# Opening of a two-model kernel in four steps of two channel blocks

## What is computed

```python
c_act = silu(c)                                   # c: one vector of 1024
mod = c_act @ w_ada[l] + b_ada[l]                 # 1024 -> 6 * 1024
sh_m, sc_m, gt_m, sh_f, sc_f, gt_f = split(mod, 6)
h = rms_norm(x, g_pre_mix[l]) * (1.0 + sc_m) + sh_m
proj = h @ w_in[l]                                # 1024 -> 3656
mq, mk, mv, dq, dk, dv, qi, ki, wi = split(proj)  # 512 * 6, 512, 64, 8
...                                               # rope on q and k; moba attention on m*,
...                                               # top-k scores from qi, ki, wi, then dsa attention on d*
x = x + gt_m * rms_norm(concat(o_moba, o_dsa) @ w_out[l])
...                                               # then a convolutional gated feed-forward
```

## Time and profile before

| | us |
|---|---|
| median of 3 runs | 2640.02 (2638.87 to 2648.0) |
| the profiled execution | 2643.63 |
| its span, first to last instruction | 2641.8 |
| PE busy | 2504.3 (95%) |
| DVE busy | 1746.1 (66%) |
| ACT busy | 1073.3 (41%) |
| POOL busy | 446.3 (17%) |
| mean granted TensorE clock | 0.984 |
| DMA read | 409.68 MB, 155 GB/s over the span |

### The profile page before, as it was taken

How to read it: one execution, slowest core, us unless ns; L and a number is a source line. 1 busy time by engine, 2 the same in 40 slices (tenths; PEclk the granted TensorE clock), 3 DMA queues, 4 the chain that set the end, 5 groups by cost and what they waited for, 6 DMA issues and landing times.

```text
span 2641.8 us, 35187 instructions
## 1 busy us (share of the span) xinstructions
PE 2504.3 (95%) x13498; PEld 2092.2 (79%) x13498; DVE 1746.1 (66%) x2572; ACT 1073.3 (41%) x1818; POOL 446.3 (17%) x462
## 2 busy tenths in 40 slices
PE   4898999989999999999989999999999999999998
PEld 3677997678988878878658888888888888777997
DVE  6976886966995785776875464665565765345454
ACT  3455544456554222226745322224322224334543
POOL 1101111001121111113842112101112110000111
PEclk9999999999999999999999999999999999999999
DMA  7644785534774453551102244352343343222462
GB/s 304 208 172 146 272 307 204 206 129 175 244 266 152 159 199 135 189 185 57 63 32 72 88 170 145 144 187 89 135 168 120 141 181 117 91 73 76 156 196 95
DMA packets 118294, 413.02 MB, mean 156 GB/s; under 512 B 13552, under 2 KB 17776, under 8 KB 118128
## 3 DMA queue, kind: packets, MB, share of 16 engines
q1 hardware_dynamic: 117568, 409.06, 44.5%
q10 hardware_dynamic: 560, 1.72, 0.2%
HBM read 409.68 MB, written 1.05 MB: 155 GB/s over the span
## 4 chain that ended last, share of the span: by engine, by line
PE 61%; DVE 3%; ACT 2%; POOL 1%; issue 1%; DVEq 0%; POOLq 0%; ACTq 0%
PE ps L1102 18%; PE ps L1104 18%; PE ps L1103 18%; PE ps L1318 2%; PE ps L1295 1%; PE ps L1255 1%; PE ps L1286 1%; DVE sl L1672 1%; PE ps L1266 1%; POOL ap L2194 1%; POOL X L2155 1%; ACT F L1440 1%; DVE F L1789 1%; DVE mjunk L1686 0%; ACT sh L1381 0%
## 5 line engine op out<-in xcount | busy, mean ns | idle before, releaser
L1102 PE MATMUL ps<-hH,sh 128*128 128x256 f32 (+1 forms) x2560 | 843.0, 329 | 8.7 <-DVE hL L1760 3.5
L1103 PE MATMUL ps<-hL,sh 128*128 128x256 f32 (+1 forms) x2560 | 836.2, 327 | 0.0
L1104 PE MATMUL ps<-hH,sl 128*128 128x256 f32 (+1 forms) x2560 | 836.1, 327 | 0.0
L1672 DVE TENSOR_TENSOR sl<-raw,sh 128x1024 fp32r<-128x1024 f32 x534 | 655.1, 1251 | 123.3 <-ACT sh L1381 122.3
L1381 ACT ACTIVATE sh<-raw 128x1024 fp32r<-128x1024 f32 x534 | 540.3, 1039 | 392.5 <-PE ps L1104 326.3
L1686 DVE CUSTOM_DVE_ANT_0 mjunk<-raw,cB,V 128x1024 bf16<-128x1024 f32 x384 | 545.6, 1421 | 30.3 <-DMA C<-in_cst 8.3
L1102 PEld LDWEIGHTS ps<-hH,sh 128*128 128x128 f32 x2560 | 481.7, 188 | 61.7 <-issue 10.6
L1103 PEld LDWEIGHTS ps<-hL,sh 128*128 128x128 f32 x2560 | 482.8, 189 | 48.8 <-issue 1.7
L1104 PEld LDWEIGHTS ps<-hH,sl 128*128 128x128 f32 x2560 | 480.6, 188 | 48.1
L2167 POOL TENSOR_TENSOR uLl<-F,uHh 128x256 fp32r<-128x256 f32 (+1 forms) x132 | 166.8, 1264 | 988.9 <-ACT uHh L1561 853.5
L1102 PE MATMUL ps<-sh,uHh 128*128 128x512 f32 x792 | 316.5, 400 | 15.2 <-DVE sl L1672 15.1
(11 more groups left out here) (170 smaller groups left out, 2254.7 us busy)
## 6 DMA issues: line engine op xcount, KB each, us to landing
raw<-in_w SPq DMA_DIRECT2D x756, 512.0 KB, 4.5
raw<-in_w SPq DMA_DIRECT2D x16, 256.0 KB, 3.8
cB<-in_rpb SPq DMA_DIRECT2D x64, 64.0 KB, 2.6
X<-in_x ACTq DMA_DIRECT2D x1, 1024.0 KB, 11.7
X<-in_ctx SPq DMA_DIRECT2D x1, 1024.0 KB, 7.9
out<-X SPq DMA_DIRECT2D x2, 512.0 KB, 2.6
raw<-in_w SPq DMA_DIRECT2D x2, 288.0 KB, 5.5
cB<-in_c ACTq DMA_DIRECT2D x1, 512.0 KB, 5.5
```

The source lines that it names most:

```text
L1102: self.e.matmul(out, lh, rh, start=start, stop=False)
L1103: self.e.matmul(out, lh, rl, start=False, stop=False)
L1104: return self.e.matmul(out, ll, rh, start=False, stop=stop)
L1672: self.e.tensor_tensor(lo[:, 0:w], raw[:, 0:w], hi[:, 0:w].bitcast(F32), ALU.subtract).then_inc(self.sems["w_lo"], 1)
```

## The change

The 16 modulation sums, the blocks of `h` and the start of the projection are interleaved in four steps kp = 0 to 3. Each step takes four sums (2kp, 2kp + 1, 8 + 2kp, 9 + 2kp), makes two channel blocks of `h` for both token tiles (`hpair`), and runs the units of these two channels for column blocks 6, 0 and 1. x is transposed once, before scale and shift, into `xT` (it lies in the space of `O1`). Block 7 comes behind block 0. The load of x moves from third in ACT's queue to first in SP's. Rates and the order of the index steps change; the `idx` steps of both tiles now come ahead of all `rank` steps, in layer 1 as well.

```diff
-RATES = {"proj0": 0.8, "proj1": 0.65, "att": 0.0, ...
+RATES = {"proj0": 1.0, "proj1": 0.65, "att0": 0.75, "att1": 0.0, ...
@@ mixer
-        begun = {cb: blocks(cb) for cb in (6, 7)}
-        for i in range(2):
+        begun = {cb: blocks(cb) for cb in (6, 7)} if l else self.opening(hid, blocks)
+        for i in range(2 if l else 0):
...
-        for cb in (6, 7, 0, 1, 2, 3, 4, 5):
+        for cb in (6, 7, 0, 1, 2, 3, 4, 5) if l else (6, 0, 7, 1, 2, 3, 4, 5):
...
-                    if at in (2, 4) and pending:
+                    if (at in (2, 4) or not l and cb in (7, 2)) and pending:
                         pending.pop(0)()
                     self.pace()
...
+                if not l:
+                    pending.insert(0, go)      # the turn of block 7 goes first
+                    continue
...
-        self.rate = RATES["att"]
+        self.rate = RATES[f"att{l}"]
+    def opening_mods(self, kp):
+        for u in (2 * kp, 2 * kp + 1, 8 + 2 * kp, 9 + 2 * kp):
+            self.jobs.remove(("w_ada", 0, u))
+            self.add("place", unit=self.unit(False, [("w_ada", 0, None, u * 128, D)], ("w_ada", 0, u)))
+
+    def opening(self, hid, blocks):
+        cbs = (6, 0, 1)
+        banks = {cb: [self.bank(), self.bank()] for cb in cbs}
+        begun = {cb: [] for cb in cbs}
+        for kp in range(4):
+            if kp:
+                self.opening_mods(kp)
+            self.add("hpair", kp=kp, hid=hid, f=self.next("F", 3))
+            for cb in cbs:
+                u = blocks(cb, (2 * kp,), banks[cb])[0]
+                begun[cb].append(u)
+                self.add("proj", tiles=[0, 1], last=True, **u)
+        return begun
@@ index_scores
-            steps += [lambda i=i: (some(i, 0), some(i, 1)), lambda i=i: (some(i, 2), some(i, 3))]
+            steps += [lambda i=i: [some(i, g2) for g2 in range(4)]]
+        for i in range(2):
             steps += [lambda i=i, lo=lo: self.add("rank", mid=mid, i=i, lo=lo, hi=lo + 2) for lo in range(0, 8, 2)]
@@ program
-        self.fill(6)
+        self.opening_mods(0)
         for t in range(2):
-            self.norm_tile(h, t, AB, 0, None, t == 1)
-            firsts.append(self.firsts.pop())
-        self.fill(10)
-        AB.append(ab1(0, 0, "g_pre_mix")())
...
+            st = self.rms_open(self.xs(t, 0), D)
+            self.rms_more(st, self.xs(t, 1))
+            self.rms_close(st, 2)
+            ys = [self.place("S", j) if t else self.next("PT", 2) for j in range(2)]
+            self.add("scale", t=t, st=st, ys=ys, xs=[self.xs(t, 0), self.xs(t, 1)])
+            for g in range(2):
+                b = self.bank()
+                self.add("xturn", src=ys[g], b=b, k0=4 * g, i=t)
+                self.left(b)
@@ Sync.start: x ahead of V and of the first eight raw loads
+        self.e.dma_start(self.m["X"][:, 0:2, :], self.dram["x"].rearrange("b (t p) d -> p (b t) d", p=P)).then_inc(
+            self.sems["ld2"], 16)
@@ Scalar: x no longer loaded here; new steps
+    def xturn(self, s):          # PE: four transposes; ACT: one copy of 128x512 from PSUM to xT
+    def hpair(self, s):
+        kp, F = s["kp"], self.buf(s["f"])
+        self.wait_ge(self.gone(s["f"]))
+        self.wait_ge(self.got("A0", kp))
+        self.wait_ge(self.own("a_ps"))
+        self.e.activation(F[:, 0:256], self.m["xT"][:, 2 * kp, :], ACT.Identity, scale=..., bias=...)
+        self.done("a_sb", ("h0_a", kp))
+        self.wait_ge(self.own("a_sb"))
+        self.wait_ge(self.got("h0_v", kp))
+        self.e.activation(self.m["hH"][:, 2 * kp:2 * kp + 2, 0:256], ..., ACT.Copy)    # 128x512
@@ Vector: new step, behind the step's four modulation sums
+    def hpair(self, s):
+        self.e.scalar_tensor_tensor(A, ..., 1.0, ..., ALU.add, ALU.mult)               # 128x2
+        for i in range(2):
+            self.wait_ge(self.got("xT", kp // 2, i))
+        self.e.tensor_scalar(F[:, 256:512], self.m["xT"][:, 2 * kp + 1, :], A[:, 1:2], B[:, 1:2], ALU.mult, ALU.add)
+        self.wait_ge(self.got("h0_a", kp))
+        self.wait_ge(self.got("h0_hi", kp))
+        self.e.tensor_tensor(self.m["hL"][:, k, 0:256], F..., self.m["hH"][...], ALU.subtract)   # 128x512
```

More of the change, by code:

```diff
@@ L1205, in turn @@
         self.done("tr", ("full", p["b"]), ("left", p["src"]))
+    def xturn(self, s):
+        self.wait_ge(self.gone(s["b"]))
+        self.wait_ge(self.got("y", s["src"]))
+        for k in range(4):
+            c = slice(k * 128, (k + 1) * 128)
+            x = self.e.transpose(self.buf(s["b"])[:, c], self.buf(s["src"])[:, c], self.m["C"][:, C_ID:C_ID + 128])
+        x.then_inc(self.sems["tr"], 1)
+        self.done("tr", ("full", s["b"]), ("left", s["src"]))
     def qturn(self, s):
@@ L1352, in __init__ @@
                           scale=self.scale, turn=self.turn, hsplit=self.hsplit, gspread=self.gspread,
[L1353 removed]
+                          xturn=self.xturn, hpair=self.hpair, pout=self.pout, qturn=self.qturn, idx=self.idx, att_e=self.att_e, att_c=self.att_c,
                           glu1_a=self.glu1_a, glu1_b=self.glu1_b, glu1_c=self.glu1_c,
@@ L1445, in turn, with xturn @@
         self.done("a_ps", ("left", p["b"]), ("h_f", p["id"]))
+    def xturn(self, s):
+        self.wait_ge(self.got("full", s["b"]))
+        self.e.copy(self.m["xT"][:, s["k0"]:s["k0"] + 4, s["i"] * 128:(s["i"] + 1) * 128],
+                    cut(self.buf(s["b"])[:, 0:1], [[128, 4], [1, 128]])).then_inc(self.sems["a_ps"], 1)
+        self.done("a_ps", ("left", s["b"]), ("xT", s["k0"] // 4, s["i"]))
+    def hpair(self, s):
[3 more added lines that the diff above has]
+        self.wait_ge(self.own("a_ps"))
+        self.e.activation(F[:, 0:256], self.m["xT"][:, 2 * kp, :], ACT.Identity, scale=self.m["A"][:, 2 * kp:2 * kp + 1],
+                          bias=self.mcol("w_ada", 0, 0, 0, 2 * kp)).then_inc(self.sems["a_sb"], 1)
+        self.done("a_sb", ("h0_a", kp))
+        self.wait_ge(self.own("a_sb"))
+        self.wait_ge(self.got("h0_v", kp))
+        self.e.activation(self.m["hH"][:, 2 * kp:2 * kp + 2, 0:256], cut(F[:, 0:1], [[256, 2], [1, 256]]),
+                          ACT.Copy).then_inc(self.sems["a_sb"], 1)
+        self.done("a_sb", ("h0_hi", kp))
     def u_free(self, s):
@@ L1699, in coef @@
         self.done("v_sb", ("A", s["id"]))
+    def hpair(self, s):
+        kp, F = s["kp"], self.buf(s["f"])
+        for k in (2 * kp, 2 * kp + 1):
+            self.wait_ge(self.got("mod", "w_ada", 0, k, 0))
+            self.wait_ge(self.got("mod", "w_ada", 0, 8 + k, 0))
+        A, B = self.m["A"][:, 2 * kp:2 * kp + 2], self.mcol("w_ada", 0, 0)[:, 2 * kp:2 * kp + 2]
+        self.e.scalar_tensor_tensor(A, self.mcol("w_ada", 0, 1)[:, 2 * kp:2 * kp + 2], 1.0,
+                                    self.vec("g_pre_mix", (0,), 2 * kp, 2), ALU.add, ALU.mult).then_inc(
+            self.sems["v_sb"], 1)
+        self.done("v_sb", ("A0", kp))
+        self.wait_ge(self.own("v_sb"))
+        self.wait_ge(self.gone(s["f"]))
+        for i in range(2):
+            self.wait_ge(self.got("xT", kp // 2, i))
+        self.e.tensor_scalar(F[:, 256:512], self.m["xT"][:, 2 * kp + 1, :], A[:, 1:2], B[:, 1:2], ALU.mult,
+                             ALU.add).then_inc(self.sems["v_sb"], 1)
+        self.done("v_sb", ("h0_v", kp))
+        self.wait_ge(self.got("h0_a", kp))
+        self.wait_ge(self.got("h0_hi", kp))
+        self.wait_ge(self.own("v_sb"))
+        k = slice(2 * kp, 2 * kp + 2)
+        self.e.tensor_tensor(self.m["hL"][:, k, 0:256], cut(F[:, 0:1], [[256, 2], [1, 256]]),
+                             self.m["hH"][:, k, 0:256].bitcast(F32), ALU.subtract).then_inc(self.sems["v_sb"], 1)
+        self.done("v_sb", ("left", s["f"]), ("h0", s["hid"], kp))
     def gcol(self, s):
```

28 lines of the change are left out of this document (12 added, 16 removed).

## The result

| | before | after |
|---|---|---|
| median of 13 runs each, us | 2640.64 (2635.62 to 2648.0) | 2650.09 (2641.74 to 2654.57) |
| ratio after / before | | 1.003, 95% interval 1.0018 to 1.0042 |
| the profiled execution, us | 2643.63 | 2650.76 |
| its span, us | 2641.8 | 2648.6 |
| mean granted TensorE clock | 0.984 | 0.980 |

The change made the kernel slower by 0.3%. That is inside the 0.5% that the prediction called no change, but the sign is the other one, and the time lies above the top of the range (2645).

A forecast was written before the change was run, and what follows sets the result against it. DVE's list was the path to 134.4 us, then PE, then both in turns, PE after 240. A lead of 5.0 us at 236 plus 0.5 in layer 1 gave 2638.1 profiled, median 2634.5; range 2622 to 2645.

The forecast's parts named there:

- H3 to P: From DVE's end of `hpair` 3 to its rope of block 3: 63.4 us, ending at 125.4, 9.0 ahead.
- P to Q: From DVE's rope of block 3 to its first dsa round: two rank steps add 1.5 us (bounds 0 and 4.4).
- the dsa rounds: From DVE's first dsa round to 202.9 us: six more sums, mostly covered, cost 2.5 us (bounds 0 and 8.2).
- Rival 2: Sums in the dsa rounds break PE's stream: 13.4 us lost against 7.5 won, 2645.4 us; chance 0.08.
- The first four sums and x: Start of the kernel: sums end at 15.9 us as before; x edit worth nothing (bounds 0 and 2.8 us loss).
- `hpair` 0: First pair of `h` blocks: sixteen transposes from 16.6 us, then copy, Identity, hH and hL, ending H0 at 22.9.
- Steps 1 to 3: Opening after `hpair` 0: steps 2 and 3 take 13.1 us each, including a 1.7 us load wait; H3 at 62.0.
- PE in the opening: Rests lower PE's clock, losing about 1.6 us per step; step 3 ends at 72.0, DVE waits 6.5 for block 6.
- Rival 3: PE stays at 1.2 GHz through the opening: 8.5 us slower, 2648.5 us; chance 0.03.
- rival 1: Full cover: loads land in time and the dsa rounds' six sums hide wholly; 15.8 us off, 2624.2 us; chance 0.15.
- rival 4: An early start buys nothing: DVE's list stays as long and waits eat the rest; 2640 us; chance 0.04.
- Layer 1's index order: Layer 1's new order of idx and rank steps ends ranks two paces sooner: 0.5 us won (bounds -2 and 2).

The follow-up runs named there:

- e9: The changed kernel with `finish` looking four weight units ahead, not counting sums, from block 7 to the output product; ratio 1.0006 to the kernel before.
- e13: The kernel before with the look-ahead counting four weight units and no sums over the same stretch; ratio 1.0001 to the kernel before.
- e3: The kernel before with only rates moved: 0.59 in the projection, 0.75 (seven sums) in layer 0's dsa rounds; ratio 1.0005 to the kernel before.
- e1: The changed kernel with rate 1.36 in the projection and 0.0 beside the dsa rounds (two sums there); ratio 1.0092 to the kernel before.
- e2: The changed kernel with rate 0.0 beside the dsa rounds, the remaining sums left to `need`; ratio 1.0031 to the kernel before.
- e10: The changed kernel with the edits of e5, e6 and e9 together; 2637.36 us, ratio 0.999 to the kernel before.
- e8: The changed kernel with the load of x back in third place of ACT's queue; ratio 1.003 to the kernel before.
- e5: The changed kernel with both token tiles' squares and statistics ahead of either scale; ratio 0.9997 to the kernel before.
- e6: The changed kernel with pending `lower` splits done before each opening step's four sums; ratio 1.0012 to the kernel before.
- e12: e10 with three sums placed ahead of DVE's wait for block 6's turn and rate 0.45 in the dsa rounds; 2633.04 us, ratio 0.9977 to before.
- e4: The kernel before with only the index steps in the new order, in both layers; ratio 1.0001 to the kernel before.
- e11: e1 with the look-ahead counting four weight units and no sums; ratio 1.0071 to the kernel before.

## Why the prediction was wrong

The prediction had the feed-forward at 231.2 (5.0 ahead) and it came at 247.6. Of these 16.4 us, 4.6 arise ahead of H0, 1.0 in the steps, 0.8 from H3 to P, 1.4 from P to Q, 8.8 from Q to O, and -0.3 behind.

**The step that failed is "the dsa rounds".** It said that six more sums cost 2.5 us there, bounds 0 to 8.2. The stretch grew by 11.3. The sums themselves cost about what was said: 3.3 in e9, or 1.5 against e13. What was missing is the other half of "of a step that is moved, every instruction counts": the sums take places in the row of units that `finish` looks along, so the splits of `w_out` moved too, and with them their loads. The prediction has no term for them: it put what the move does to the splits and loads of `w_out` at nothing, without a row. PE waits 3.0 us for `sl` while its clock is low, and the clock stays low to 189 us; e9 removes the wait and gets 8.1 us of the stretch back, 5.7 of them as PE's busy time, and 5.2 us at the feed-forward. e3 makes such waits in before by the rates alone (4.8 us), and e1 and e2 make them elsewhere (10.2 us in two waits, 16.5 in one). That the wait caused the whole of the 5.7 us of clock is not shown: e10 has no such wait and yet 4.4 us more busy time than e9.

**Rival 2 had the right place and sign, and part of the mechanism.** It priced the rounds at 13.4 us lost, and 11.3 were. It laid 8.2 of this on the sums' DVE time; e9, with all seven sums there, loses 3.3, and e1, with two, loses 7. That it comes near the time is luck. But its PE rest that brings the low level is there: the wait of 2.6 us for `PT` behind two sums, with the clock low from 206.55 to 213.1.

**The first four sums and x: right in effect.** The sums end at 16.76 instead of 15.9, since x's megabyte is ahead of them (first sum at 11.17, in e8 at 8.33), well within the 2.8 us bound. Worth of the x edit: 0, as e8 says.

**`hpair` 0: wrong by 4.6 us.** "Sixteen transposes from 16.6" took both scales as ready. Tile 1's statistics were not: the steps of the new order put its squares behind tile 0's copies on ACT. In before ACT had no copies between the two tiles' squares, and DVE's scale of tile 1 stood at 19.92 with a wait of 0.74, in after at 22.28. e5 removes 3.9 of the 4.6. The Identity of 128x256, taken as 0.45, is 0.60; DVE's half is 0.41, not 0.3.

**Steps 1 to 3: right in size.** 12.9, 13.1 and 13.1 were predicted; they took 12.7, 13.3 and 14.1. The DMA wait was to be 1.7 in steps 2 and 3; it was 2.09 and 3.04, each in two parts, since the third sum of each step waited once more (0.98 and 0.96), where the prediction had the later three follow without a wait. e6 takes both away.

**PE in the opening: the clock was kinder than forecast.** After rests of 4.30 and 4.60 us (ahead of 29.09 and 53.62) PE came back at 1.2 GHz for 7 and 13 products, after rests of 1.33 and 2.95 (40.38 and 67.79) at 2.4. Step 3 took 8.3 us for 36 matmuls instead of 10.0, so DVE's wait for block 6 was 4.58 and not 6.5:

```profile
84.66 0.69 DVE L1930 TENSOR_SCALAR qkT<-ps 128x512 f32<-128x512 f32 x1 [4.58 <-PE ps L1256]
```

Rival 3, the low clock throughout, did not happen. Nor did rival 1: neither the loads nor the dsa rounds were covered. Against rival 4, an early start that buys nothing, stands e12, whose total is 6 us below before.

**From H3 to P: right** (64.1 us, 63.4 predicted); the 1.9 us less of waiting is paid elsewhere in the stretch. **P to Q: too low by 1.4.** +2.9 against before, 1.5 predicted, inside the bounds. DVE is busy 19.97 of 22.13 us in block 4, and PE waits 2.8 us once for `PT` there and runs at a clock of 0.85, where in before it was 1.00. **Layer 1's index order: 0** (e4; 0.5 predicted).

**Behind 240 us.** In the profiled pair after has 11.35 us to make up at the feed-forward and ends 6.8 behind in span. From there to the end the 14 profiled kernels take 2392 to 2412 us, before 2405.6 and after 2401.0; the four that keep the old opening (before, e3, e4, e13) have a mean of 2400.0, the eight with the new one (all but e1 and e11) 2397.9. Part of the spread is one long stretch of the second model, from the idle matmuls at about 1360 to those at about 2440: 1072.5 us in after, 1072.8 in e3 and 1077.0 in before, of the same work. So whether a lead of under about 5 us at 240 reaches the end can't be read off one profile, and the ratio of many runs is the better witness: 7.9 us for after (interval 4.8 to 11.1), where its marks say 11.4.

## What to carry to other kernels

Where a planner places prefetches by counting entries of a list, moving any other entries of that list moves the prefetches: list what each step issues before and after the move, and look at the first consumer behind the moved block. Price a wait of PE with two terms, the rest and the clock behind it, and give the second a range: with waits equal to within 0.7 us it differed by 4.4 us here (e9, e10). And before pricing a chain, check on each engine what is written ahead of its first link: one statistic, written behind two copies, cost 3.9 us of the opening (e5).

## What the runs showed of the hardware

- Rests of PE of nearly one length did different things to the granted clock: 2.95 us before 67.79 left it at 2.4 GHz, a rest of 2.60 left it there for 1.5 us in e9 (low from 203.3 to 206.7) and had it at 1.2 at once in e10 (198.96 to 204.9). In e3 rests of 2.48 (before 178.00) and 2.60 (before 201.75) left it at 2.4 GHz, and one of 2.35 (before 187.26) had it at 1.2 for seven products. Between e9 and e10, with waits of 6.9 and 7.6 us, the clock made 4.4 us of PE time in one stretch of 40.
- The same 1.05 MB of x landed by 9.65 us when first in SP's queue and by 13.54 when third in ACT's, and held the first sum from 8.33 to 11.17. The fourth sum ended only 0.8 us later (16.76 against 15.99): behind x the four sums followed each other at 1.44 us from start to start, while in e8 the second and third waited 0.93 and 1.43 us for their loads.
